# Three split buffers and one ring of raw slots for the weights and the late w_ada blocks

## The reference, cut to what matters

```python
m_lat = jnp.split(silu(c) @ w_ada + b_ada, 6, axis=-1)     # shift, scale, gate; twice
m_ctx = jnp.split(silu(c_ctx) @ w_ada + b_ada, 6, axis=-1)
a_lat = modulate(rms_norm(x, norm_mix), m_lat[0], m_lat[1])
a_ctx = modulate(rms_norm(ctx, norm_mix), m_ctx[0], m_ctx[1])
q, v, g = split(a @ w_in)                                  # 2048 x 6144
z = einsum('bld,wdk->wblk', a, w_f)                        # 2 x 2048 x 2048, clipped to +-30
# 16 heads, both directions: chunked scan with decay f(z), keys 1 - f, state from the context
h = x + m_lat[2] * ((rms_norm(o) * silu(g)) @ w_o)
t = modulate(rms_norm(h, norm_ffn), m_lat[3], m_lat[4])
out = rms_norm(h + m_lat[5] * ((silu(t @ w_gate) * (t @ w_up)) @ w_down), final_norm)
```

## Time and profile before

| | us |
|---|---|
| median of 3 runs | 1967.49 |
| lowest and highest | 1964.05 and 1968.95 |
| the profiled execution | 1960.22 |
| its span, first to last instruction | 1958.4 |
| PE busy in it | 1858.6 (95%) |
| DVE busy | 1255.5 (64%) |
| ACT busy | 870.0 (44%) |
| mean granted TensorE clock | 0.988 of full speed |

### The profile page before, as it was taken

One profiled execution on the slowest core, in us unless ns is written; L12 is line 12 of the kernel. 1 busy time (PEld: TensorE's weight loads), 2 busy tenths in 40 slices (PEclk: granted clock), 3 DMA queues, 4 the chain that ended last, 5 costly groups with the idle time before them and its releaser, 6 DMA issues.

```text
span 1958.4 us, 31877 instructions
## 1 busy us (share of the span) xinstructions
PE 1858.6 (95%) x13318; PEld 1692.7 (86%) x13318; DVE 1255.5 (64%) x1949; ACT 870.0 (44%) x1186; POOL 0.2 (0%) x4
## 2 busy tenths in 40 slices
PE   6989999999999999999889999999999999999998
PEld 2248989788989788888889989999999999999996
DVE  4754668796978787878984456555555555444445
ACT  4482435354545354545444444333333333344444
POOL 0000000000000000000000000000000000000000
PEclk9999999999999999999899999999999999999999
DMA  8964444453443444343555546777767676555552
GB/s 323 383 235 155 158 129 140 141 162 130 140 140 129 141 160 131 127 144 127 189 181 193 184 127 184 225 216 221 220 206 224 217 215 203 173 183 183 183 183 108
DMA packets 175378, 353.20 MB, mean 180 GB/s; under 512 B 12737, under 2 KB 80642, under 8 KB 174594
## 3 DMA queue, kind: packets, MB, share of 16 engines
q1 hardware_dynamic: 175042, 351.11, 54.8%
q10 hardware_dynamic: 192, 0.05, 0.0%
HBM read 346.92 MB, written 4.19 MB: 179 GB/s over the span
## 4 chain that ended last, share of the span: by engine, by line
PE 76%; DVE 16%; issue 3%; ACT 3%; DMA 2%; ACTq 0%; SPq 0%; DVEq 0%
PE bank L1117 18%; PE bank L1119 18%; PE bank L1118 18%; DVE wlo L686 3%; DVE aacc L778 3%; PE score L1222 2%; PE bank L1154 2%; PE bank L1155 2%; PE bank L1156 2%; DVE work L832 2%; PE score L1117 1%; PE score L1118 1%; PE score L1119 1%; DVE work L862 1%; DVE work L831 1%
## 5 line engine op out<-in xcount | busy, mean ns | idle before, releaser
L686 DVE TENSOR_TENSOR wlo<-raw,whi 128x1024 fp32r<-128x1024 f32 x496 | 607.2, 1225 | 560.2 <-ACT whi L423 559.6
L1117 PE MATMUL bank<-ahi,whi 128*128 128x256 f32 (+1 forms) x2912 | 894.7, 307 | 42.5 <-DVE wlo L686 17.5
L423 ACT ACTIVATE whi<-raw 128x1024 fp32r<-128x1024 f32 x496 | 525.2, 1060 | 889.0 <-PE bank L1119 651.4
L1118 PE MATMUL bank<-alo,whi 128*128 128x256 f32 (+1 forms) x2912 | 884.6, 304 | 0.0
L1119 PE MATMUL bank<-ahi,wlo 128*128 128x256 f32 (+1 forms) x2912 | 884.4, 304 | 0.0
L1117 PEld LDWEIGHTS bank<-ahi,whi 128*128 128x128 f32 x2912 | 561.8, 193 | 73.2 <-DVE wlo L686 22.0
L1119 PEld LDWEIGHTS bank<-ahi,wlo 128*128 128x128 f32 x2912 | 561.7, 193 | 21.1
L1118 PEld LDWEIGHTS bank<-alo,whi 128*128 128x128 f32 x2912 | 562.2, 193 | 18.9
L1154 PE MATMUL bank<-whi,ahi 128*128 128x256 f32 x512 | 150.4, 294 | 16.5 <-DVE arena L788 9.9
L778 DVE SCALAR_TENSOR_TENSOR aacc<-aw,cs,aacc 128x1024 f32<-128x1024 f32 x120 | 153.7, 1281 | 4.3 <-DMA aw<-in_w_ada_dram 3.6
L1155 PE MATMUL bank<-wlo,ahi 128*128 128x256 f32 x512 | 145.6, 284 | 0.0
(11 more groups left out here) (222 smaller groups left out, 1740.8 us busy)
## 6 DMA issues: line engine op xcount, KB each, us to landing
aw<-in_w_ada_dram SPq DMA_DIRECT2D x134, 512.0 KB, 4.8
raw<-in_ffn_w_gate_dram SPq DMA_DIRECT2D x88, 512.0 KB, 3.8
raw<-in_ffn_w_up_dram SPq DMA_DIRECT2D x88, 512.0 KB, 3.7
raw<-in_ffn_w_down_dram SPq DMA_DIRECT2D x88, 512.0 KB, 3.4
raw<-in_hg_w_in_dram SPq DMA_DIRECT2D x128, 256.0 KB, 3.0
raw<-in_hg_w_f_dram SPq DMA_DIRECT2D x128, 256.0 KB, 3.1
raw<-in_w_ada_dram SPq DMA_DIRECT2D x40, 512.0 KB, 6.4
raw<-in_hg_w_in_dram SPq DMA_DIRECT2D x32, 512.0 KB, 3.9
```

What stands on the lines that cost most here:

```text
L423: act.activation(whi[:, ck % SPL, :], raw[:, ck % RAW, :], ACT.Copy).then_inc(s_hi, 1)
L686: dve.tensor_tensor(wlo[:, ck % SPL, :], raw[:, ck % RAW, :], whi[:, ck % SPL, :].bitcast(F32), ALU.subtract).then_inc(s_lo, 1)
L1117: pe.matmul(dst, w, ah, start=start, stop=False, skip_group_check=True)
L1118: pe.matmul(dst, w, al, start=False, stop=False, skip_group_check=True)
```

## The change

1. SPL goes from 2 to 3. `whi` and `wlo` have three buffers each, and `hi(ck)` waits for chunk ck - 3 instead of ck - 2.
2. The buffer `aw` is gone. The late blocks of w_ada go through the same four slots of `raw` as the chunks. `RING` lists all loads in the order in which DVE takes them (chunk ck, then the `ada` blocks of that position), `SEQ` gives the place q of each, the slot is q % 4, and the load waits until DVE is done with the block four places earlier, be it a chunk (`s_lo`) or an `ada` block (`s_ac`).
3. The direct blocks have 6 slots instead of 8.
4. The first `ada` block stands at position 9 instead of 4, so that all of e = 0 lie in positions 9 to 32. The other positions are as before.

```diff
-SPL = 2
+SPL = 3
-DIRECT = 8
+DIRECT = 6
...
+            def slot_free(kind, n):
+                q = SEQ[kind, n]
+                if q >= RAW:
+                    before, m = RING[q - RAW]
+                    sp.wait_ge(s_lo if before == "w" else s_ac, m + 1)
+                return q % RAW
+
+            def load_ada(i):
+                slot = slot_free("a", i)
+                e, k = divmod(i, KD)
+                whole(slot, raw[:, slot, :], wada[k, :, 2 * D + e * CW:2 * D + (e + 1) * CW])
...
             for ck in range(C_B, CHUNKS):
                 load(ck)
-                for i in ada_loads(ck):
-                    if i < 2:
-                        sp.wait_ge(s_du, len(DIRECT_ADA))
-                    else:
-                        sp.wait_ge(s_ac, i - 1)
...
+                for i in ada_blocks(ck):
+                    load_ada(i)
...
             def hi(ck):
-                act.wait_ge(s_raw[ck % RAW], raw_landed(ck))
+                q = SEQ["w", ck]
+                act.wait_ge(s_raw[q % RAW], landed(q))
                 if ck >= SPL:
                     act.wait_ge(s_used, ck - SPL + 1)
...
             def ada(i):
-                dve.wait_ge(s_aw[i % 2], 16 * (i // 2 + 1))
+                q = SEQ["a", i]
+                block = raw[:, q % RAW, :]
+                dve.wait_ge(s_raw[q % RAW], landed(q))
...
-    begin = ADA_ENDS[e - 1] + 1 if e else 4
+    begin = ADA_ENDS[e - 1] + 1 if e else KD // 2 + 1
...
+RING = []
+for _ck in range(CHUNKS):
+    RING.append(("w", _ck))
+    RING += [("a", _i) for _i in ada_blocks(_ck)]
+SEQ = {block: q for q, block in enumerate(RING)}
```

More of the change, by code:

```diff
@@ L161, in build @@
         fsum = rstd[0:1, 0:T]
-        aw = sb("aw", [P, 2, CW])
         aacc = sb("aacc", [P, CW])
         dslot = ([work[:, KD * TT + i * CW:KD * TT + (i + 1) * CW] for i in range(3)]
-                 + [arena[:, 4 * D + 2 * P + i * CW:4 * D + 2 * P + (i + 1) * CW] for i in range(3)]
-                 + [aw[:, i, :] for i in range(2)])
+                 + [arena[:, 4 * D + 2 * P + i * CW:4 * D + 2 * P + (i + 1) * CW] for i in range(3)])
         yhi = ahi[:, 0:2, T:TT]
@@ L230, in build @@
         s_used = sem("chunk_used")
-        s_aw = [sem(f"aw_in{i}") for i in range(2)]
         s_ac = sem("ada_accumulated")
@@ L306, in whole @@
                 sp.dma_start(dst, src).then_inc(s_raw[slot], 16)
+            def slot_free(kind, n):
[8 more added lines that the diff above has]
+                whole(slot, raw[:, slot, :], wada[k, :, 2 * D + e * CW:2 * D + (e + 1) * CW])
             def load(ck):
-                if ck >= RAW:
-                    sp.wait_ge(s_lo, ck - RAW + 1)
-                slot = ck % RAW
+                slot = slot_free("w", ck)
                 dst = raw[:, slot, :]
@@ L419, in hi @@
             def hi(ck):
-                act.wait_ge(s_raw[ck % RAW], raw_landed(ck))
+                q = SEQ["w", ck]
+                act.wait_ge(s_raw[q % RAW], landed(q))
                 if ck >= SPL:
                     act.wait_ge(s_used, ck - SPL + 1)
-                act.activation(whi[:, ck % SPL, :], raw[:, ck % RAW, :], ACT.Copy).then_inc(s_hi, 1)
+                act.activation(whi[:, ck % SPL, :], raw[:, q % RAW, :], ACT.Copy).then_inc(s_hi, 1)
             for r, v in ((R_C, c[0]), (R_CCTX, c_ctx), (R_NMIX, norm_mix[0]), (R_NFFN, norm_ffn[0]), (R_FIN, final_norm),
@@ L685, in lo @@
                 dve.wait_ge(s_hi, ck + 1)
-                dve.tensor_tensor(wlo[:, ck % SPL, :], raw[:, ck % RAW, :], whi[:, ck % SPL, :].bitcast(F32),
+                dve.tensor_tensor(wlo[:, ck % SPL, :], raw[:, SEQ["w", ck] % RAW, :], whi[:, ck % SPL, :].bitcast(F32),
                                   ALU.subtract).then_inc(s_lo, 1)
@@ L1317, in _ @@
                     last.then_inc(s_ft, 1)
-def raw_landed(ck):
-    return sum(32 if C_B <= c < C_G else 16 for c in range(ck % RAW, ck + 1, RAW))
 ADA_ENDS = (34, 54, 82, 102, 131, 150)
@@ L1338, in ada_blocks, with landed @@
     return [i for i in range(PADA) if ada_chunk(i) == ck]
-def ada_loads(ck):
-    return [i for i in range(PADA) if (ada_chunk(i - 2) + 5 if i >= 2 else C_B + 5) == ck]
+RING = []
[3 more added lines that the diff above has]
+SEQ = {block: q for q, block in enumerate(RING)}
+def landed(q):
+    return sum(32 if RING[n][0] == "w" and C_B <= RING[n][1] < C_G else 16 for n in range(q % RAW, q + 1, RAW))
 def ada_ends(ck):
```

6 lines of the change are left out of this document (2 added, 4 removed).

## The result

The changed kernel takes 1943.81 us (median of 4; 1940.58 to 1945.54), the kernel before 1967.05 in the same comparison: a ratio of 0.9881, interval 0.9862 to 0.9901. A second comparison gave 1944.93 and 0.9890 (0.9869 to 0.9911). The forecast was 1957.2 with a range from 1966.5 down to 1950.0: right that it is faster, wrong in the size, which is twice as large. Over all executions of the study the medians are 1965.6 (60 of before) and 1944.5 (8 of after): 21.1 us, where 10.3 were forecast. The two profiled executions differ by 17.8 us (1960.22 and 1942.41).

A forecast was written before the change was run, and what follows sets the result against it. PE was busy 95% of the span, so gains could come only where it waits, mostly for DVE. Terms 4.8 + 1.5 + 0 + 1.4 + 1.6 + 0.5 + 0.5 = 10.3 us off 1967.5 gave 1957.2, range 1950 to 1966.5.

The forecast's parts named there:

- the floor of 0.85 us: PE's waits for values: 0.85 us taken as the least wait, set by DVE's copy itself, so it would remain.
- the zero for the G chunks: G chunks: DVE is busy 12.00 of 12.00 us and is the bound, so another buffer gives it no time; 0 us.
- the prologue's 0.5: Prologue: part of ACT's 1.31 us wait for PE may go, between 0 and 1.3 us; 0.5 taken.
- first Z chunks, wait: First Z chunks: moving the ada blocks cuts PE's wait for values from 4.04 to 0.85 us; gain 3.2 us.
- first Z chunks, clock: First Z chunks: with the shorter wait PE's clock does not fall afterwards; gain 1.6 us.
- second pair: Second pair: the third buffer lets DVE run ahead, and PE's wait for values falls from 2.35 to 0.85 us; gain 1.5.
- pairs 3 to 8: Later pairs: DVE is late from its own work after score waits, so the third buffer gains nothing; 0 us.
- FFN start, w_down, small waits: Third buffer removes PE's waits for alo (1.4 us), the evacuation at w_down (1.6) and two small lo waits (0.5).
- the bounds +1.0 and -2: G chunks: between 1.0 us gained from the lost wait for aw and 2 us lost to late ring loads.
- scan waits shrink too: Rival: a one-chunk lead carries past the score waits, about 22 us more gained, 1935; chance 0.10.
- only the moved blocks count: Rival: the third buffer's gains do not come, only the moved ada blocks gain, 3 to 6 us, 1963; chance 0.22.
- The slow ring: Rival: in the G chunks ring loads land too late and stretch DVE; 20 us lost at 9.6 us landings, 1977; chance 0.10.

The follow-up runs named there:

- the runs that take one part away: Changed kernel with two split buffers only in the prologue (1947.23 us), pairs (1947.68 us) or from the G chunks on (1951.70 us); throughout, 1957.55 us.
- two in the pairs: Changed kernel with ACT's conversion waiting as with two split buffers in the eight pairs only, three elsewhere; 1947.68 us.
- ring and two buffers: Changed kernel with two split buffers in place of three, throughout (1957.55 us) or only from the G chunks on (1951.70 us).
- values first: Changed kernel with DVE doing the copies of values and the clipping of the gates ahead of a position's w_ada block; 1937.15 us, ratio 0.9852.
- both edits: Changed kernel with copies and clip ahead of the w_ada block, and w_ada blocks placed earlier so the G chunks have none; 1935.10 us, ratio 0.9842.

## Why the prediction was wrong in size

The places were right in the main and the sizes were not. By the runs that take one part away, the moved blocks gave 6.5 us where 4.8 were forecast, and the ring with the direct slots 1.6 where nothing was. The third buffer gave 13.1 where its terms add up to 5.5: 2.7 for 0.5 in the prologue, 3.2 for 1.5 in the pairs, 7.2 for 3.5 from the G chunks on. Four steps failed: the floor of 0.85 us, the price of a wait, the zero for the G chunks, and the clock that was left out of the terms; and the prologue's 0.5 was too small. By profiles, stage by stage:

| term | forecast | measured | from |
|---|---|---|---|
| first Z chunks, wait | 3.2 | 3.7 | this part of pair 1, 50.4 to 45.0, less the clock |
| first Z chunks, clock | 1.6 | 1.7, in the second profile 3.4 | granted clock |
| second pair | 1.5 | 2.5 | 89.7 to 87.1 |
| pairs 3 to 8 | 0 | 0 in waits | two in the pairs |
| G chunks | 0 | 2.2 (third buffer 1.5) | means of 3 and of 5 profiles |
| FFN start, w_down, small waits | 1.4 + 1.6 + 0.5 | 5.3 | 772.0 to 766.7 |
| prologue | 0.5 | 1.7, uncertain by 0.7 | means of 5 and of 8 |
| sum | 10.3 | 17.1 | |

**The floor.** The step "What is late next is the copy itself: the least wait that PE shows at the same point of a pair is 0.85 us, where DVE was idle in time" failed. DVE was not idle there: a block of 1.28 us ended just before the copy. In before, ahead of the wait at 454.84:

```profile
452.90 1.28 DVE L778 SCALAR_TENSOR_TENSOR aacc<-aw,cs,aacc 128x1024 f32<-128x1024 f32 x1
454.10 1.28 DVE L814 COPY arena<-bank 128x512 f32<-128x512 f32 x2
```

DVE goes from the block to the copy without a break. In the two pairs 0.1 us of idle time remains each time, so 0.75 us was subtracted twice that came off as well.

**What a wait costs.** The forecast took the idle time in the brackets for the price. PE's matmuls overlap; the row ahead of the wait at 1175.62 starts at 1174.86, and matmuls of this form start every 0.12 us:

```profile
1174.86 0.28 PE L1119 MATMUL bank<-ahi,wlo 128*128 128x256 f32 x1
...
1175.81 0.28 PE L1118 MATMUL bank<-alo,whi 128*128 128x256 f32 x1
```

From start to start it is 0.76, less 0.12, and the next comes 0.07 late: 0.71 us lost for a wait shown as 0.47. Counting matmuls says it without any modelled end. Sixteen us of before that hold the two other waits for `alo` (0.48 each), then sixteen of after without any, both at full clock:

```profile
1177.00:1193.00 16.00, 15.04 (x124) 14.70 (x123) 12.76 (x24) 8.60 (x14) 0.00 (x0) 1.00 0.58 172
```
```profile
1163.00:1179.00 16.00, 16.00 (x135) 16.00 (x135) 13.33 (x22) 8.79 (x14) 0.00 (x0) 1.00 0.69 196
```

Eleven matmuls fewer, 1.3 us at 0.12 each, though PE is shown idle for 0.96. So each wait costs 0.2 to 0.25 us more than its row: for the six waits from the FFN on 1.2 to 1.5 us of the 1.8 that were missing. In pair 2 the same count from start to start gives 2.6 for the 2.35, of which 0.3 remain.

**The G chunks.** "A buffer more gives it no time" was right for DVE and blind for ACT. In before:

```profile
1038.68 1.06 ACT L423 ACTIVATE whi<-raw 128x1024 fp32r<-128x1024 f32 x1 [3.30 <-PE bank L1119]
...
1043.45 0.38 ACT L567 ACTIVATE rstd<-ob 128x256 f32<-128x256 f32 x1
```

ACT waited 3.30 us for PE to free a split buffer and then worked without a break until the norm's row (L567), for which PE stood 0.99 us. With three buffers the same chain of rows is there (from 1023.14), but PE does not wait for the norm's row. Of the bounds +1.0 and -2 the value came out beyond the better end. The third buffer's part is 1.5 us (mean of two profiles with ring and two buffers, 153.8, against 152.3). The ring's own part is then 0.7, in a column that is spread over 2; that the lost wait for `aw` gave it, less what the late loads took, would fit but is not shown.

**The prologue.** 0.5 was taken between 0 and 1.3; 1.7 is over that range, though its uncertainty reaches the 1.3. Which wait of the prologue it comes from was not taken apart.

**The medians.** "None of the terms depends on what makes it 7 us longer" failed. The share of the granted clock below full, times the span, is 26.2 us as a mean over the 56 executions of before whose clock is on record and 18.7 over the 8 of after. If PE had work in all of that time, it is 7.5 of the 21.1, where 1.6 were forecast. In the profiles this difference lies in pair 1 (3.4 and 5.1 us in before, 1.4 and none in after) and in the G chunks (8.5 and 5.1 against 5.1 and 3.4), so it is partly in the terms above. With the mean of both profiles of before and the mean of the eleven with the blocks moved and four raw slots (88.1 to 80.9) that term alone is 7.2, and the sum 18.9. Of the last 2.2 us, 0.6 lie behind the last column (18.8 and 19.8 us against 18.7 twice); the rest has no place. It is within the interval of the second comparison, and that of the first starts 0.6 us above 18.9.

**The range.** Its lower end was added up too high: with the terms that the prediction names for it (ring -2, second pair 0.5, clock 0) the gain is 5.7 us, not 7. This changes nothing in the result, which lies past the other end.

**Held:** pairs 3 to 8, rows for L819 and L793 unchanged; no wait for `alo` behind the first, none for the evacuation at w_down. The mechanism in the pairs was as forecast too, DVE's waits for `hi` turning into longer waits for scores. DVE's waits in the eight pairs, before (130 to 910 us) and after (127 to 900):

```profile
DVE wlo L686 <- ACT whi L423: 94.0, 46, 4.4
DVE work L858 <- PE score L1225: 21.4, 10, 2.9
```
```profile
DVE wlo L689 <- ACT whi L426: 41.2, 27, 4.2
DVE work L863 <- PE score L1230: 59.0, 11, 8.3
```

The rival "scan waits shrink too" came out at nothing. The rival "only the moved blocks count" has its own kernel, 1959. The slow ring is real in the G chunks, and hidden but for about 0.5 us (1.06 less 0.61) in this profile.

## What to carry over

Read the rows directly ahead of the row that seems to be a floor: a floor is only one where the releasing engine stood idle. Price a wait of a pipelined engine from start to start, or by counting instructions in equal stretches, and look at every engine that a deeper buffer frees, the one that converts too. And work moved off a late place pays only where it lands in a stage whose bound is another engine: sixteen or seventeen blocks cost 14 us in the pairs (10 with values first), 10 in the G chunks and about 1 at w_o.

## What the runs showed of the hardware

Which waits of PE are followed by a stretch at 1.2 GHz is a matter of odds. Over all fourteen profiles, between 130 and 900 us: with 37 of 46 waits of 2.6 to 2.9 us such a stretch began in the wait or within 2 us behind it, with one of 8 of 2.2 to 2.4 us, with 11 of 29 of 1.6 to 2.0 us. The same wait of the same kernel had one and had none (354.26 in before had none, its like in the second profile had one). By the lengths of otherwise equal pairs most cost 1.2 to 1.7 us, about half as much again as the wait. The Trainium skill ("TensorE: Matmul & The Clock Gate", section "What's actually happening") says that an idle engine falls to half its clock and that activity releases it; the traces agree for 37 of these 46 long waits and show no sharp bound. Kernels with shorter waits lost less at the lower clock, as means over their executions: 26.2 us before, 18.7 after, 14.0 with values first, 11.1 with both edits.

The start of the groups varies by 3.6 us between profiles of kernels that are the same up to there, where DMA is at its full share; a term of 1 us in such a stage can't be read from one profile.
